# Delta-rule layer of a two-layer decoder trunk: the order of work at the ends of the head groups

## What is computed

```python
h = x @ gdn_w_in                                   # q, k, v, z: 12 heads x 128 each; a, b; q_mem
qkv = silu(causal_depthwise_conv(h[..., :3 * MIX_WIDTH], conv_w))          # 4 taps
q, k = l2_normalize(q), l2_normalize(k);  g = -exp(a_log) * softplus(a + dt);  beta = sigmoid(b)
# in 4 chunks of 64 tokens, per head:
a = I + strict(kb k' * decay);  u, w = a^-1 (v * beta), a^-1 (kb * exp(gc))    # kb = k * beta
v_new = u - w @ state;  o = q_dec @ state + (tril(q k' * decay)) @ v_new
state = state * g_last + k_dec' @ v_new
o = rms_norm(o) * silu(z)
x = layer_norm(alpha * x + concat([o, memory_attention(q_mem)]) @ w_out)
x = layer_norm(alpha * x + square(relu(x @ w1)) @ w2)
```

## Time and profile before

| | |
|---|---|
| time, median of 3 runs | 2470.22 us (2469.14 to 2471.08) |
| profiled execution, its own time | 2471.89 us |
| its span, first to last instruction | 2470.1 us |
| mean granted TensorE clock | 0.986 |
| DVE busy | 1467.5 us, 59% |
| ACT busy | 1071.8 us, 43% |
| GpSimd busy | 247.9 us, 10% |
| HBM read | 412.77 MB, 168 GB/s over the span |

### The profile page before, as it was taken

The page is one execution under the profiler, slowest core; times in us unless marked ns, Lnnn a source line. Parts: engine busy times, 40 slices in busy tenths (PEclk is TensorE's granted clock), DMA queues, the critical chain, the costliest instruction groups (busy, mean ns, idle before and its releaser), DMA issues.

```text
span 2470.1 us, 35483 instructions
## 1 busy us (share of the span) xinstructions
PE 2384.2 (97%) x13572; PEld 2078.7 (84%) x13577; DVE 1467.5 (59%) x1550; ACT 1071.8 (43%) x1340; POOL 247.9 (10%) x221
## 2 busy tenths in 40 slices
PE   8999989999999999999999999989899999999997
PEld 7897778888888888889899898978788888888885
DVE  6654567546555556577756757545865554555555
ACT  4455444434444444354535435333443443443443
POOL 0150001001000001000122320310010000000000
PEclk9999999999999999999999999999999999999999
DMA  6662456565566565655424324126455665656654
GB/s 233 188 187 94 137 172 200 199 193 188 192 185 196 192 191 182 200 190 162 137 69 139 108 79 154 60 90 226 140 188 195 184 196 196 187 190 195 188 191 158
DMA packets 234624, 417.10 MB, mean 169 GB/s; under 512 B 23761, under 2 KB 42474, under 8 KB 232938
## 3 DMA queue, kind: packets, MB, share of 16 engines
q1 hardware_dynamic: 233114, 410.73, 52.2%
q10 hardware_dynamic: 1360, 4.19, 0.4%
HBM read 412.77 MB, written 2.10 MB: 168 GB/s over the span
## 4 chain that ended last, share of the span: by engine, by line
PE 48%; issue 40%; DVE 5%; POOL 4%; ACT 2%; DMA 1%; SPq 0%; POOLq 0%; ACTq 0%; DVEq 0%
PE quad L563 10%; PE quad L592 6%; PE quad L590 6%; PE quad L591 6%; PE quad L566 5%; PE quad L534 3%; PE quad L536 3%; PE quad L538 3%; DVE cv L1793 2%; POOL hl L2070 1%; ACT whi L1036 1%; PE quad L947 1%; PE quad L934 1%; DVE wlo L1413 1%; PE quad L944 1%
## 5 line engine op out<-in xcount | busy, mean ns | idle before, releaser
L1413 DVE TENSOR_TENSOR wlo<-raw,whi 128x1024 fp32r<-128x1024 f32 x760 | 979.1, 1297 | 726.1 <-ACT whi L1036 724.0
L1036 ACT ACTIVATE whi<-raw 128x1024 fp32r<-128x1024 f32 x760 | 798.7, 1058 | 979.7 <-PE quad L592 525.8
L563 PE MATMUL quad<-xs,whi 128*128 128x512 f32 x2048 | 649.9, 397 | 7.4 <-DVE xs L1673 3.7
L590 PE MATMUL quad<-whi,hh 128*128 128x512 f32 x1344 | 528.9, 393 | 5.2 <-DVE hl L1548 3.7
L592 PE MATMUL quad<-whi,hl 128*128 128x512 f32 x1344 | 523.8, 390 | 0.0
L591 PE MATMUL quad<-wlo,hh 128*128 128x512 f32 x1344 | 523.5, 390 | 0.0
L566 PEld LDWEIGHTS quad<-xs,wlo 128*128 128x128 f32 x2048 | 386.7, 189 | 91.0
L566 PE MATMUL quad<-xs,wlo 128*128 128x256 f32 x2048 | 403.8, 279 | 0.0
L563 PEld LDWEIGHTS quad<-xs,whi 128*128 128x128 f32 x2048 | 314.6, 190 | 10.0 <-DVE wlo L1413 5.5
L590 PEld LDWEIGHTS quad<-whi,hh 128*128 128x128 f32 x1344 | 252.7, 188 | 60.0 <-issue 7.2
L592 PEld LDWEIGHTS quad<-whi,hl 128*128 128x128 f32 x1344 | 252.5, 188 | 53.1
(11 more groups left out here) (286 smaller groups left out, 2103.4 us busy)
## 6 DMA issues: line engine op xcount, KB each, us to landing
raw<-in_mlp_w SPq DMA_DIRECT2D x512, 512.0 KB
raw<-in_gdn_w_in SPq DMA_DIRECT2D x105, 512.0 KB
raw<-in_w_out SPq DMA_DIRECT2D x64, 512.0 KB
raw<-in_mem_w_kv SPq DMA_DIRECT2D x32, 512.0 KB
raw<-in_mla_w_in SPq DMA_DIRECT2D x25, 512.0 KB
raw<-in_mla_w_ukv SPq DMA_DIRECT2D x24, 256.0 KB
gb<-in_ln_g SPq DMA_DIRECT2D x4, 1024.0 KB, 6.5
gb<-in_ln_b SPq DMA_DIRECT2D x4, 1024.0 KB, 8.5
```

The source lines that it names most:

```text
L563: last = nc.tensor.matmul(both, b.whi[:, slot, k, cols], b.xs[:, :, kt, :], start=start, stop=stop, skip_group_check=True)
L590: nc.tensor.matmul(ps[:, t, 0:n], ah[:, kt, toks], hi[:, k, 0:n], start=start, stop=False)
L1036: nc.scalar.activation(b.whi[:, c % NSPLIT], b.raw[:, slot], ACT.Copy).then_inc(sem.hi_ready, 1)
L1413: nc.vector.tensor_tensor(b.wlo[:, c % NSPLIT], b.raw[:, c % NRAW], b.whi[:, c % NSPLIT].bitcast(F32), ALU.subtract).then_inc(sem.lo_ready, 1)
```

## The change

At the end of groups 0 and 1, ACT and DVE take up the next group's q panel (`conv(g + 1, 0)`) inside `gdn(g)`: DVE runs its taps ahead of the scale of the rows, ACT ahead of the rows' split. TensorE runs four chunks of the next k panel ahead of the rows' turns, not three. One split of a chunk moves from behind the k panel's `conv` to before its tanh on both engines. ACT copies `kbt` out ahead of the tanh of v. DVE writes the first rows of `vn` directly from PSUM, ahead of both `uu` copies, and TensorE's waits for `uu` move to the first products that overwrite those banks. After the last group, TensorE starts the memory heads and `out1` at once; the last rows are scaled in step 0 of that attention, turned after step 2's chunk, into the banks of the `qm1` panel, and split in step 3; chunks from 4 on wait for them. The number of instructions, splits and loads is the same. The core of the diff:

```diff
             # TensorE
-            def turn(g, src, kts):
-
+            def turn(g, src, kts, bank=None):
+
+                ps = turn_ps[g % 2] if bank is None else bank
...
             def out1_chunk(ci):

+                if 2 * ci >= 2 * GH:
+                    pe.wait_ge(sem.turn_lo, TURN_AT["ln1_1"])
...
+            def out1_step(i):
+
+                if i < NH // CK:
+                    out1_chunk(i)
+                if i == 1:
+                    pe.wait_ge(sem.a_o, HG * NC)
+                if i == 2:
+                    pe.wait_ge(sem.panel_free, PANEL_AT["qm1"] + 1)
+                    turn_rows(HG - 1, [panel_ps[PANEL_AT["qm1"] % 2][:, k, :] for k in range(2)])
...
                 for t in tiles:
                     pe.wait_ge(sem.a_w, n0 + t + 1)
-                    pe.wait_ge(sem.d_u, n0 + t + 1)
...
+                        if j == 2:
+                            pe.wait_ge(sem.d_u, n0 + 2)
                         for h in range(GH):
                             nc.tensor.matmul(side_ps[t][r, h * P:(h + 1) * P], b.qdt[:, t, h, r], state[:, h, :],
...
+                    if j == 0:
+                        pe.wait_ge(sem.d_u, n0 + 1)
                     each(lambda h, o, s_: nc.tensor.matmul(o[r, :], b.aq[r, t, h, r], b.vn[r, 0, h, :],
...
                 beside(g, 6 + LEVELS - 1 + NC)
-                if g < HG - 1:
-                    turned_panel(f"k{g + 1}", 0, 3)
+                if g == HG - 1:
+                    return
+                turned_panel(f"k{g + 1}", 0, 4)
+                turn_rows(g, turn_ps)
+
+            def turn_rows(g, banks):
+
                 pe.wait_ge(sem.or_set, g + 1)
                 for k in range(2):
-                    turn(TURN_AT[f"gdn{g}"] + k, b.orow[:, :].rearrange("p t h c -> p (t h c)"), 2 * k)
+                    turn(TURN_AT[f"gdn{g}"] + k, b.orow[:, :].rearrange("p t h c -> p (t h c)"), 2 * k,
+                         banks[(TURN_AT[f"gdn{g}"] + k) % 2])
...
-                    turned_panel(name, 3 if g and i == 1 else 0, place)
+                    turned_panel(name, 4 if g and i == 1 else 0, place)
...
-            pe.wait_ge(sem.turn_lo, TURN_AT["ln1_1"])
+            pe.wait_ge(sem.turn_lo, TURN_AT[f"gdn{HG - 1}"])
             pe.wait_ge(sem.panel_free, PANEL_AT["out1"])
-            attention(NH + NM, mem_heads, lambda i: out1_chunk(i) if i < NH // CK else None)
+            attention(NH + NM, mem_heads, out1_step)
...
             # ScalarE (ACT)
-            def attention(n0, n, fed_from, fed_steps):
+            def attention(n0, n, fed_from, fed_steps, at=lambda i: None):
                 for i in range(n0, n0 + n + 3):
+                    at(i - n0)
                     if n0 <= i - 2 < n0 + n:
                         probs_out(i - 2)
...
                     for t in range(TT):
                         act.wait_ge(sem.p_kt, n0 + t + 1)
                         bank_out(b.kt, t, turn_ps, sem.a_kt)
+                    for t in range(TT):
+                        act.wait_ge(sem.p_kbt, n0 + t + 1)
+                        bank_out(b.kbt, t, side_ps, sem.a_kbt)

                 conv(g, 2, keys_out)
-                for t in range(TT):
-                    act.wait_ge(sem.p_kbt, n0 + t + 1)
-                    bank_out(b.kbt, t, side_ps, sem.a_kbt)
                 feed(1)
...
-                feed(1 if g == HG - 1 else 2)
+                feed(1)
+                if g == HG - 1:
+                    return
+                conv(g + 1, 0, lambda: feed(1))
+                feed(1)
                 for k in range(2):
                     split_turn(TURN_AT[f"gdn{g}"] + k, b.hh, g * GH + 2 * k)
...
-                feed(2 if g else 0)
-                conv(g, 0)
+                if g:
+                    feed(1)
+                else:
+                    conv(0, 0)
                 feed(PANEL - 1 - early)
                 rows_out(g, 0)
                 feed(1)
-                conv(g, 1)
-                feed(PANEL // 2 + 1)
+                conv(g, 1, lambda: feed(1))
+                feed(PANEL // 2)
...
             take_t("qm1", 0, b.qm, 0, scale_mem)
-            attention(NH + NM, NM, 0, NH // CK)
+
+            def rows_hi(i):
+                if i == 3:
+                    for k in range(2):
+                        split_turn(TURN_AT[f"gdn{HG - 1}"] + k, b.hh, (HG - 1) * GH + 2 * k)
+
+            attention(NH + NM, NM, 0, NH // CK, rows_hi)
...
             # VectorE (DVE); turn_out takes a bank, as turn does
                     if n0 <= i - 1 < n0 + n:
                         divide(i - 1)
+                    at(i - n0)
                     if i - 3 >= n0:
                         head_lo(i - 3)
...
-            def conv(g, i, splits=0):
+            def conv(g, i, splits=0, between=lambda: None):
...
                 last.then_inc(sem.conv1, 1)
+                between()
                 feed(splits)
                 dve.wait_ge(sem.tanh1, m + 1)
...
+                dve.wait_ge(sem.p_u, n0 + 1)
+                nc.vector.tensor_copy(b.vn[0:CHUNK, 0].rearrange("p h c -> p (h c)"),
+                                      side_ps[0][0:CHUNK, :]).then_inc(sem.d_vn, 1)
                 for t in range(TT):
                     dve.wait_ge(sem.p_u, n0 + t + 1)
                     nc.vector.tensor_copy(b.uu[:, t].rearrange("p h c -> p (h c)"), side_ps[t][:, :]).then_inc(sem.d_u, 1)
...
-                    if j == 0:
-                        dve.wait_ge(sem.d_u, n0 + 1)
-                        nc.vector.tensor_copy(vn, uu).then_inc(sem.d_vn, 1)
-                    else:
+                    if j:
                         dve.wait_ge(sem.p_vn, g * (NC - 1) + j)
-                        if j == 2:
-                            dve.wait_ge(sem.d_u, n0 + 2)
+                        if j != 3:
+                            dve.wait_ge(sem.d_u, n0 + t + 1)
...
-                dve.wait_ge(sem.o_rs, g + 1)
-                times(b.orow[:, :, :, :], b.orow[:, :, :, :], factor(2)).then_inc(sem.or_set, 1)
-                if g < HG - 1:
-                    feed(1)
-                for k in range(2):
-                    turn_out(TURN_AT[f"gdn{g}"] + k, 0, gain=lambda kt: vcol(1, 8))
+
+                def scaled():
+                    dve.wait_ge(sem.o_rs, g + 1)
+                    times(b.orow[:, :, :, :], b.orow[:, :, :, :], factor(2)).then_inc(sem.or_set, 1)
+
+                def turned_out(banks):
+                    for k in range(2):
+                        turn_out(TURN_AT[f"gdn{g}"] + k, 0, gain=lambda kt: vcol(1, 8), bank=banks[k])
+
+                if g == HG - 1:
+                    return scaled, turned_out
+                conv(g + 1, 0, 1, scaled)
+                feed(1)
+                turned_out([turn_ps[(TURN_AT[f"gdn{g}"] + k) % 2] for k in range(2)])
...
-                feed(2 if g else 0)
-                conv(g, 0)
+                if g:
+                    feed(1)
+                else:
+                    conv(0, 0)
                 feed(PANEL - early)
-                conv(g, 1)
-                feed(5)
+                conv(g, 1, 1)
+                feed(4)
...
-                gdn(g)
-            attention(NH + NM, NM, 0, NH // CK)
+                last_group = gdn(g)
+
+            def rows_step(i):
+                scaled, turned_out = last_group
+                if i == 0:
+                    scaled()
+                if i == 2:
+                    turned_out([panel_ps[PANEL_AT["qm1"] % 2][:, (TURN_AT[f"gdn{HG - 1}"] + k) % 2, :] for k in range(2)])
+
+            attention(NH + NM, NM, 0, NH // CK, rows_step)
```

More of the change, by code:

```diff
@@ L630, in turn @@
                         kt = kts + i
-                        last = nc.tensor.transpose(turn_ps[g % 2][:, (i * TT + t) * P:(i * TT + t + 1) * P],
+                        last = nc.tensor.transpose(ps[:, (i * TT + t) * P:(i * TT + t + 1) * P],
                                                    src[:, t, kt * P:(kt + 1) * P], b.ident[:, :])
@@ L980, in gdn @@
                 beside(g, 6 + LEVELS - 1 + NC)
-                if g < HG - 1:
-                    turned_panel(f"k{g + 1}", 0, 3)
+                if g == HG - 1:
[3 more added lines that the diff above has]
+            def turn_rows(g, banks):
                 pe.wait_ge(sem.or_set, g + 1)
                 for k in range(2):
-                    turn(TURN_AT[f"gdn{g}"] + k, b.orow[:, :].rearrange("p t h c -> p t (h c)"), 2 * k)
+                    turn(TURN_AT[f"gdn{g}"] + k, b.orow[:, :].rearrange("p t h c -> p t (h c)"), 2 * k,
+                         banks[(TURN_AT[f"gdn{g}"] + k) % 2])
             turned_panel("q0", 0, 1)
@@ L1422, in feed, with turn_out @@
                         fed[0] += 1
-            def turn_out(g, kt, gain=None, bias=None):
+            def turn_out(g, kt, gain=None, bias=None, bank=None):
+                ps = turn_ps[g % 2] if bank is None else bank
                 dve.wait_ge(sem.turned, g + 1)
@@ L1429, in turn_out @@
                 if gain is None:
```

(6 more changed lines are left out.)

## The result

The changed kernel takes 2440.83 us (median of 4 runs, 2439.76 to 2443.28), the kernel before 2470.65 us on the same chip (4 runs). The ratio is 0.988, 95% interval 0.9863 to 0.9897: 29.8 us less, between 25.5 and 33.8. The forecast was 2442 us, 28 us less. The profiled execution took 2443.28 us, its span is 2441.6 us (before: 2471.89 and 2470.1).

A forecast was written before the change was run, and what follows sets the result against it. TensorE, busy 2384 of 2470.1 us, was taken as the bound; only gaps and clock could be won. Gaps 20.1 plus clock 8.8 gave 28.9, less 0.9 for margins: 2470.2 - 28 = 2442 us, range 2438 to 2452.

The forecast's parts named there:

- The q panel: Boundaries of groups 0 to 1 and 1 to 2: TensorE's two 2.67 us waits for `cv` go; gain 5.3 us, clock 2.5.
- rival D: Both boundaries: scale behind q taps on DVE delays TensorE's turns; 30.6 us lost against 28, so 2473 us; chance 0.02.
- The moved split: DVE's `wlo` for chunk v4 comes straight behind the taps; two TensorE waits go, gain 1.5 us.
- Scaled keys: ACT copies `kbt` before the tanh of v; TensorE's waits over three groups go, gain 3.6 us, clock 1.7.
- First rows of `vn`: DVE's `vn` copy runs about 2 us earlier; TensorE's 1.20 us wait per group goes, gain 3.6 us, clock 3.4.
- The last group: Waits of 6.0 and 3.3 us go, new 2.4 and 0.8 us come; gain 6.1 us, clock 2.9.
- Rival C: Last group: shared port makes GpSimd's two `hl` subtractions, beside a DVE split, end 1.2 us later; 2443 us; chance 0.15.
- The clock: Five stretches at the 1.2 GHz level behind gaps, 10.5 us; one of 1.7 us stays behind the new gap, gain 8.8.
- Rival B: Gaps close but low clock stretches fall behind the remaining gaps; gain about 20 us, so 2450 us; chance 0.13.
- The 0.9 us taken off: Deducted from the summed gain of 28.9 us because margins of 0.6 us could easily turn into waits; leaves 28.

## Why the prediction was right

The time lies 1.2 us from the forecast, and the mechanism is the one that was forecast: the listed waits went, two small ones came where they were expected, and the clock followed. That the number is so close is partly luck, as the end of this section adds up. Point by point:

- *The q panel.* Both waits of 2.67 us went. The scale came 2.1 us before TensorE, as worked out, and k6 0.8 us before it instead of 0.6. Nothing waits on `or_set`: rival D has no place, and the margin was measured with three chunks (0.7 us of waiting each) and with more work on DVE (0.35 us each).
- *The moved split.* Term 1.5 us, and the waits did go; alone it moves 3.7 us of waits, because the load behind it comes earlier too. The prediction priced the split at its own waits alone. In the whole change the surplus falls on waits that the keys' part removes too, so the sum did not suffer.
- *Scaled keys.* 3.6 us went. `qd_set` did not become late; alone, without the split, it does by 0.6 us.
- *First rows of `vn`.* 3.6 us went, by itself too.
- *The last group.* Forecast: a gap of 2.4 us and a wait of 0.8. Measured: 2.36 and 1.25. The prediction's working had the low halves 0.2 us late and put 0.8; they were 1.2 late. Rows show two causes: GpSimd's subtractions took 3.06 us for 2.49, the first of them beside a split of DVE, and ACT took up the rows 3.8 us behind the start of the turns, not the 3.2 us of the working. Rival C was right in kind and half in size on this side (0.57 us for 1.2).
- *The clock.* 8.8 us were forecast net. Between 1150 and 1700 us it is that in the first profile: five low stretches became one, 10.5 less 1.7. In the second profile of the same kernel none is left there. Rival B, by which it would not come back, did not happen; but its premise holds, that where a stretch falls is chance. The extra stretch at 1073 us took 1.7 us back in both.
- *The 0.9 us taken off* for small margins were not needed.

One term was missing. In the stage, waits fell by 19.6 us and the clock gave 8.8, 28.4 together, but the stage is 30.4 us shorter. The second profile, with no low stretch in the stage, says the same: 563.5 - 531.3 = 32.2 us, where 19.6 + 10.5 = 30.1 are accounted for. A likely cause is how the profile counts an idle stretch. Rows of the kernel before, around a listed gap of 0.35 us:

```profile
1187.90 0.28 PE L536 MATMUL quad<-xs,whi 128*128 128x256 f32 x1
1188.02 0.28 PE L538 MATMUL quad<-xs,wlo 128*128 128x256 f32 x1
1188.65 0.39 PE L534 MATMUL quad<-xs,whi 128*128 128x256 f32 x1 [0.35 <-DVE wlo L1413]
```

In a full stream one matmul starts 0.12 us behind the other, though each is drawn 0.28 us long. Behind the gap the start comes 0.63 us later, so the stream lost 0.51 us where 0.35 are listed: 0.16 more. The gaps of 2.67 us at 1329.42 and of 5.95 us at 1625.86 lose 0.16 more too. Twelve gaps went and two came; if each counts like these, 10 x 0.16 = 1.6 us of the 2.0 that are missing. This was worked out from rows, not tried by a run of its own.

For the profiled execution the errors against the 28 us then add up so: waits 0.5 us less than forecast (19.6 for 20.1), the 0.9 us not needed, 2.0 us from the missing term, 1.7 us lost at 1073 us, and 0.2 elsewhere: 28 - 0.5 + 0.9 + 2.0 - 1.7 - 0.2 = 28.5 us of span. Each is small beside the gain, and they nearly cancel.

## What to carry to other kernels

When one engine is nearly always busy, list its gaps, follow each to the engine that is late, and look there for work that could stand behind instead of ahead; then work out the new margin of every step that the moved work now stands before, since margins of 0.6 to 2.1 us at the group boundaries held here within 0.2 us (the one at the last group, worked out over three engines, was 1 us off). Parts that each close a gap add up nearly, but one part can remove or uncover the waits of another; price the clock stretches behind each gap as chance, and look for waits that a slow clock has hidden. Count a gap by the starts around it, not by the idle time alone.

## What the runs showed that was not expected

**A low clock hides waits.** With `vn` alone, TensorE's waits on `wlo` rose from 1.5 to 2.6 us though nothing about the splits had changed and the clock there had not fallen (1.00 for 0.66). The likely reading: in the kernel before, the low stretch had cost TensorE some 2.5 us of matmul time just ahead of v4, more than the 1.12 us of the wait that it hid.

**GpSimd's work cost DVE more than itself.** In the changed kernel's step 3, DVE's two products of the probabilities (SBUF in and out) beside GpSimd's subtractions at 1617.34 us:

```profile
1612.69 0.62 DVE L1577 TENSOR_SCALAR prob<-prob,rinv 128x256 f32<-128x256 f32 x2
...
1618.71 1.84 DVE L1577 TENSOR_SCALAR prob<-prob,rinv 128x256 f32<-128x256 f32 x2
```

1.84 us for what takes 0.62 alone, and GpSimd 3.06 for 2.49. The prediction had the delay on GpSimd's side, 1.2 us; 0.57 fell there and 1.2 on DVE. The Trainium skill ("SBUF — State Buffer", on the shared port pair) says that a DVE operation with two SBUF inputs, or one in a two-port mode, which it says `tensor_scalar` can enter, and a GpSimd operation that reads SBUF exclude each other, and that whichever starts first blocks the other for its whole instruction. The trace agrees: DVE's split had begun first (1616.78 us) and the first subtraction was late, the subtractions had begun before the products and these were late. That the products ran in a two-port mode is shown by no row.

**The same gap costs 1.7 us or nothing.** The wait of 2.36 or 2.37 us ahead of the scores had a low stretch behind it in one execution of the changed kernel and none in another.
